# A decoder step on one core: order of work at the tail of the convolution and in the last two output chunks

## What is computed

```
def conv_module(h, hist, w_pw1, b_pw1, w_dw, b_dw, g_ln, b_ln, w_pw2, b_pw2):
    a = h @ w_pw1 + b_pw1
    u = a[..., :D_MODEL] * jax.nn.sigmoid(a[..., D_MODEL:])
    ext = jnp.concatenate([hist.astype(u.dtype), u], axis=1)
    v = depthwise convolution of ext over time, 31 taps, + b_dw
    v = layernorm(v, g_ln, b_ln)
    y = jax.nn.silu(v) @ w_pw2 + b_pw2
    return y, ext[:, -(CONV_WIDTH - 1):]
...
        x = x + squared_relu_mlp(rmsnorm(x, g_ffn[l]), w_up[l], w_down[l])
...
    return rmsnorm(x, g_final), ...
```

## Time and profile before

| what | value |
|---|---|
| median of 3 executions | 1405.34 us |
| the profiled execution, its own time | 1393.17 us |
| its span from first to last instruction | 1391.2 us |
| TensorE busy | 1354.7 us, 97% |
| VectorE busy | 810.8 us, 58% |
| ScalarE busy | 601.3 us, 43% |
| GpSimd busy | 725.7 us, 52% |
| mean granted clock of TensorE | 0.99 of full |

### The profile page before, as it was taken

The page is one execution under the profiler, slowest core; times in us unless marked ns, Lnnn a source line. Parts: engine busy times, 40 slices in busy tenths (PEclk is TensorE's granted clock), DMA queues, the critical chain, the costliest instruction groups (busy, mean ns, idle before and its releaser), DMA issues.

```text
span 1391.2 us, 26303 instructions
## 1 busy us (share of the span) xinstructions
PE 1354.7 (97%) x11048; PEld 1261.1 (91%) x11048; DVE 810.8 (58%) x1232; ACT 601.3 (43%) x1021; POOL 725.7 (52%) x505
## 2 busy tenths in 40 slices
PE   7999889999999999999999999999999999999997
PEld 7877489999999999999899867678999999999997
DVE  6689557655545463766556656554685463645434
ACT  5121255443434443444666544342464444443432
POOL 3321153587878785333323444330437788887831
PEclk9999789999999999999999999999999999999999
DMA  5755302222233324332111477770223322222221
GB/s 215 209 149 147 109 31 92 92 92 91 92 100 100 104 92 147 128 92 66 35 35 53 182 296 261 269 260 7 92 75 101 98 92 92 92 91 92 91 91 65
DMA packets 108356, 160.66 MB, mean 115 GB/s; under 512 B 7696, under 2 KB 93968, under 8 KB 102992
## 3 DMA queue, kind: packets, MB, share of 16 engines
q1 hardware_dynamic: 100688, 116.50, 26.4%
q0 software_dynamic: 7168, 41.95, 8.0%
q10 hardware_dynamic: 384, 0.55, 0.1%
HBM read 146.22 MB, written 4.03 MB: 108 GB/s over the span
## 4 chain that ended last, share of the span: by engine, by line
PE 91%; DVE 4%; ACT 1%; issue 1%; DMA 1%; POOL 1%; ACTq 0%; POOLq 0%; SPq 0%; DVEq 0%
PE ps L1675 31%; PE ps L1805 21%; PE ps L1793 18%; PE ps L1935 5%; PE ps L1975 3%; PE ps L1713 2%; PE ps L2024 2%; PE ps L1726 1%; PE ps L2091 1%; ACT wh L717 1%; PE ps L2005 1%; POOL wl L589 1%; PE ps L2015 1%; PE ps L2033 0%; PE ps L1763 0%
## 5 line engine op out<-in xcount | busy, mean ns | idle before, releaser
L589 POOL TENSOR_TENSOR wl<-raw,wh 128x512 fp32r<-128x512 f32 (+2 forms) x252 | 438.0, 1740 | 441.8 <-ACT wh L717 441.6
L717 ACT ACTIVATE wh<-raw 128x512 fp32r<-128x512 f32 (+2 forms) x253 | 192.6, 762 | 386.3 <-PE ps L1675 184.5
L1675 PE MATMUL ps<-xh,wh 128*128 128x272 f32 x704 | 148.4, 292 | 12.6 <-DVE xl L1084 10.0
L589 POOL TENSOR_TENSOR wl<-wuv,wh 128x512 fp32r<-128x512 f32 x104 | 135.0, 1310 | 48.2 <-ACT wh L717 48.1
L1805 PE MATMUL ps<-mh,wh 128*128 128x272 f32 x768 | 158.7, 288 | 0.0
L1805 PE MATMUL ps<-mh,wl 128*128 128x272 f32 x768 | 158.6, 288 | 0.0
L1805 PE MATMUL ps<-ml,wh 128*128 128x272 f32 x768 | 158.3, 288 | 0.0
L1675 PE MATMUL ps<-xh,wl 128*128 128x272 f32 x704 | 145.6, 289 | 0.0
L1675 PE MATMUL ps<-xl,wh 128*128 128x272 f32 x704 | 145.4, 288 | 0.0
L1675 PEld LDWEIGHTS ps<-xh,wh 128*128 128x128 f32 x704 | 110.6, 190 | 17.7 <-POOL wl L589 9.9
L1805 PEld LDWEIGHTS ps<-ml,wh 128*128 128x128 f32 x768 | 120.4, 188 | 0.0
(11 more groups left out here) (315 smaller groups left out, 3029.3 us busy)
## 6 DMA issues: line engine op xcount, KB each, us to landing
raw<-w_up SPq DMA_DIRECT2D x32, 1024.0 KB, 5.4
raw<-w_down SPq DMA_DIRECT2D x32, 1024.0 KB, 5.1
raw<-w_pw SPq DMA_DIRECT2D x11, 1024.0 KB, 5.8
shifted<-ext SPq DMA_DIRECT2D x112, 66.5 KB, 2.0
raw<-w_o SPq DMA_DIRECT2D x4, 1024.0 KB, 5.7
raw<-w_dq SPq DMA_DIRECT2D x3, 1024.0 KB, 5.4
raw<-w_uq SPq DMA_DIRECT2D x4, 768.0 KB, 4.7
diag<-diags SPq DMA_DIRECT2D x7, 384.0 KB, 3.5
```

Of the source, the lines that this page charges most:

```text
L589: pf.tensor_tensor(weight(wl, u), weight_raw(u), f32(weight(wh, u)), ALU.subtract).then_inc(w_lo, 1)
L717: af.activation(weight(wh, u), weight_raw(u), ACT.Copy).then_inc(w_hi, 1)
L1675: m = tf.matmul(ps[:, bank_of(u) + bank, 0:width], w[:, k, :], a[:, k, part], start=(k == 0 and n == 0), stop=(k == nk - 1 and n == 2))
```

## The change

Five edits. (1) `pe_steps` gives chunk 6 seven steps (28 taps) on TensorE instead of six, so VectorE has three taps left of it. (2) At chunk 7 VectorE does `gates(7)` first, then the taps of chunk 4, then `gated(7)`, then the statistics of chunk 4; ScalarE makes the squares of chunks 4, 5 and 6 after it has issued its shift DMAs, and the next two weight copies after those. (3) TensorE's first sums (`first_sums`) move in front of the last step of chunk 7's taps. (4) The four last halves go in the order (0,0), (0,1), (1,0), (1,1); the column sums of half 0 stand within (1,1), its broadcast after it, and VectorE scales all 8 chunks of half 0 after the last addition. (5) `y` is stored two chunks at a time.

```diff
         def pe_steps(c):
-            return PE_TAPS // GROUPS if c < DC - 1 else STEPS
+            return PE_TAPS // GROUPS + max(c - (DC - LATER), 0)
...
             for h in range(2):
-                for c in range(DC):
-                    sp.wait_ge(y_out, h * DC + c + 1)
-                    sp.dma_start(o_y[:, c, PARTS[h]], yo[:, c, PARTS[h]]).then_inc(s_out, 16)
+                for c in range(0, DC, 2):
+                    sp.wait_ge(y_out, h * DC + c + 2)
+                    sp.dma_start(o_y[:, c:c + 2, PARTS[h]], yo[:, c:c + 2, PARTS[h]]).then_inc(s_out, 16)
...
                 if c == 0:
                     ahead(1)
-                else:
+                elif c < DC - 1:
                     squares_after(c - LATER)
                     ahead(2 * c)
...
-                if c > 0:
+                if 0 < c < DC - 1:
                     ahead(2 * c + 1)
-            squares_after(DC - LATER)
+            for c in range(DC - LATER - 1, DC - 1):
+                squares_after(c)
+            for u in (2 * DC - 2, 2 * DC - 1):
+                ahead(u)
...
                 k = c - LATER
-                if k >= 0:
+                if c == DC - 1:
+                    gates(c)
                     psum_taps(k)
-                    if k == EARLY:
-                        early_mean()
+                    gated(c)
                     statistics(k)
...
+            def first_sums():
+                pe.wait_ge(stat_in, 1)
+                small_part(5, 0, acc)
+                small_part(5, 1, acc2).then_inc(small_mm, 1)
+                mean_part(acc, True, False)
...
                 for k in range(n):
+                    if c == DC - 1 and k == n - 1:
+                        first_sums()
...
             last_x(0, 0)
+            last_x(0, 1)
             last_x(1, 0)
-            last_x(0, 1)
             last_recip(0)
-            dve.wait_ge(y_in, 2 * DC - 2 + 2)
+            last_x(1, 1)
+            dve.wait_ge(y_in, 2 * DC + 1)
             dve.wait_ge(f_mm, 2)
-            outputs(0, range(3))
-            last_x(1, 1)
-            outputs(0, range(3, DC))
+            outputs(0, range(DC))
...
             last_half(0, 0)
+            last_half(0, 1)
             last_half(1, 0)
-            last_half(0, 1)
-            pe.wait_ge(sq_used, SQUARES)
-            column_sums(0, acc, True, False)
-            pe.wait_ge(last_sq, 2)
-            column_sums(0, sq[:, SQUARES % 2, :], False, False)
-            column_sums(0, sq[:, (SQUARES + 1) % 2, :], False, True).then_inc(f_mm, 1)
             last_half(1, 1, DC // 2)
+            broadcast(0)
```

More of the change, by code:

```diff
@@ L575, in _ @@
             for h in range(2):
-                for c in range(DC):
-                    sp.wait_ge(y_out, h * DC + c + 1)
-                    sp.dma_start(o_y[:, c, PARTS[h]], yo[:, c, PARTS[h]]).then_inc(s_out, 16)
-            sp.wait_ge(s_out, 64 + 32 * DC)
+                for c in range(0, DC, 2):
+                    sp.wait_ge(y_out, h * DC + c + 2)
+                    sp.dma_start(o_y[:, c:c + 2, PARTS[h]], yo[:, c:c + 2, PARTS[h]]).then_inc(s_out, 16)
+            sp.wait_ge(s_out, 64 + 16 * DC)
         @block.gpsimd
@@ L788, in _ @@
             load_roots()
-            for c in range(DC - LATER + 1, DC):
-                squares_after(c)
+            squares_after(DC - 1)
             root_in()
@@ L1041, in last_squared @@
             def last_squared(i, h):
-                act.wait_ge(last_in, 2 * h + i + 1)
+                act.wait_ge(last_in, 2 * i + h + 1)
                 af.activation(last_square(i, h), x[:, DC - 2 + i, PARTS[h]], ACT.Square).then_inc(last_sq, 1)
@@ L1053, in _ @@
             act.wait_ge(sq_used, SQUARES)
[L1054 to L1058, removed]
+            for i, h in ((0, 0), (0, 1), (1, 0)):
+                last_squared(i, h)
+                last_scaled(i, h)
             last_root(0)
@@ L1153, in dve_taps @@
                 dst = v[:, c, 0:NP]
-                for k in range(PE_TAPS, TAPS):
+                first = GROUPS * pe_steps(c)
+                for k in range(first, TAPS):
                     w, a = V("w_dw", c * TAPS + k), ext[:, c, k:k + NP]
-                    if k == PE_TAPS:
+                    if k == first:
                         link(df.tensor_scalar(dst, a, w, None, ALU.mult))
@@ L1213, in _ @@
                 k = c - LATER
-                if k >= 0:
+                if c == DC - 1:
+                    gates(c)
                     psum_taps(k)
-                    if k == EARLY:
-                        early_mean()
+                    gated(c)
                     statistics(k)
-                gates(c)
-                gated(c)
+                else:
+                    if k >= 0:
+                        psum_taps(k)
+                        if k == EARLY:
+                            early_mean()
+                        statistics(k)
+                    gates(c)
+                    gated(c)
                 sample_taps(c)
@@ L1618, in last_x @@
             def last_x(i, h):
-                dve.wait_ge(last_mm, 2 * h + i + 1)
+                dve.wait_ge(last_mm, 2 * i + h + 1)
                 xp = x[:, DC - 2 + i, PARTS[h]]
@@ L1702, in run, with mean_part, small_part @@
                         sums()
+            def mean_part(a, begin, end):
+                for h in range(2):
+                    m = tf.matmul(ps[:, 6 + h, 0:HALF], invd[:, :], a[:, h * HALF:(h + 1) * HALF], start=begin, stop=end)
+                return m
+            def small_part(bank, at, a):
+                for j, b in enumerate(blocks5):
+                    m = tf.matmul(ps[:, bank, at + 2 * j:at + 2 * j + 1], a[:, b], invd[:, 0:1], start=True, stop=True)
+                return m
+            def first_sums():
[3 more added lines that the diff above has]
+                mean_part(acc, True, False)
             def tap_products(c):
@@ L1754, in _ @@
             tap_products(DC - 1)
[L1756 to L1769, removed]
             pe.wait_ge(sq_src, DC)
@@ L2088, in last_half @@
                     if k == at:
-                        broadcast(0)
+                        pe.wait_ge(last_sq, 3)
+                        column_sums(0, acc, True, False)
+                        column_sums(0, sq[:, SQUARES % 2, :], False, False)
+                        column_sums(0, sq[:, (SQUARES + 1) % 2, :], False, True).then_inc(f_mm, 1)
                     for n, (w, a) in enumerate(((wh, ah), (wh, al), (wl, ah))):
```

## The result

The changed kernel takes 1409.31 us (median of 15 executions, 1406.73 to 1413.68) against 1403.57 us of the kernel before beside it (15 executions, 1399.15 to 1410.27): ratio 1.0044, 95% interval 1.003 to 1.0057, so +4.2 to +8.0 us about a middle of 6. The medians lie 5.7 us apart. A second measurement of both kernels gave 1.0036 (1.0019 to 1.0053). The forecast was +3.7.

A forecast was written before the change was run, and what follows sets the result against it. The prediction took TensorE, holding 91% of the chain of waits, as the bound: convolution +4.2 us and tail -0.55 us sum to +3.7 us, which on a median of 1405.3 gives 1409.0 us, range 1399 to 1414.

The forecast's parts named there:

- the wait that the forecast was built on: Convolution: VectorE stands until ScalarE's square of chunk 4 is done, 5.5 us lost.
- Gates and shift: Chunk 7: VectorE idles 3.1 us before the gates, ext is written at 139.25, the shift starts 2.5 us earlier.
- The square behind the DMAs: ScalarE's shift issues hold chunk 4's square 6.68 us; VectorE loses 5.5 us; stat_in comes at 161.0, not 156.8.
- The clock: TensorE runs at the lower level from before the first sums; second sums take 4.06 us; convolution +4.2 us.
- My bound of +1.3 for the upper level: Convolution's cost if TensorE's clock stays at its upper level: sums done at 170.8, +1.3 us.
- The rest costs nothing.: From 192 to 1366 us, same instructions in the same order, costed at nothing.
- The tail: Last 25 us: reordered halves and paired stores give -0.55 us, bounds 0 and -1.1.
- Rival 1: TensorE's clock does not fall, or returns at once, in the 5.6 us wait: +0.75 us, 1406.1 us; chance 0.20.
- rival 2: ScalarE's DMA issue does not hold the square: -4.75 us with the tail, 1400.6 us; chance 0.14.
- Rival 3: ScalarE's shift issues take longer than before, 13.7 us for eight: +10.7 us, 1416.0 us; chance 0.10.

The follow-up runs named there:

- e12: The kernel before with only chunk 6's seventh tap step moved to TensorE: 0.9957 (0.9941 to 0.9972), 1394.31 against 1400.27 us.
- e4: The changed kernel, but VectorE adds the square of chunk 4 two steps later: 0.9987 (0.9975 to 1.0000) against the kernel before.
- e11: The changed kernel, but ScalarE squares chunk 4 ahead of its shift DMAs: 0.9984 (0.9968 to 0.9999) against the kernel before.
- e3: The kernel before, unchanged, run again as a control: 0.9995 (0.9979 to 1.0011).
- e9: The kernel before, unchanged, one execution for its profile alone; no ratio given, taken where the kernel before has a median of 1394.3 us.
- e2: The kernel before with only the new order of last halves and the paired stores: 0.9997 (0.9981 to 1.0013).
- e8: The changed kernel itself, measured again: 1.0036 (1.0019 to 1.0053) against the kernel before, 1408.75 us.
- e1: The changed kernel without its last-halves and store edits, so only the convolution's: 1.0044 (1.0028 to 1.0059), 1400.66 against 1393.72 us.
- e5: The changed kernel with the first sums back behind all of chunk 7's taps: 1.0014 (0.9998 to 1.0030) against the kernel before, 1406.55 us.
- e6: The changed kernel with chunk 4's square added later on VectorE and first sums behind all taps: 0.9971 (0.9956 to 0.9986), 1399.87 against 1405.17 us.
- e7: The changed kernel with chunk 6 back at six tap steps on TensorE: 1.0034 (1.0017 to 1.0051) against the kernel before, 1409.04 us.

## Why the prediction was right, and where it was not

The measured +5.7 lies on the side forecast, and the wait that the forecast was built on is there. That the time itself (1409.0 forecast, 1409.3 measured) came out so near is luck: the kernel before had its median 1.8 us lower beside the changed one than in the three executions that I built on, and of the sum's terms one was too large and one was missing. By its steps:

- *Gates and shift.* 3.1 us of idle time forecast, 3.19 measured; `ext` written at 139.25 forecast, 139.85 measured with the trace 0.45 behind. Right. What I did not see is that the second product of chunk 7, done at 137.3, is the floor, the earliest moment at which `gated(7)` can begin: edit 1 alone reaches the same start of the shift (e12), so edit 2's order gained nothing there and cost the stall.
- *The square behind the DMAs.* Right in mechanism, and shown by e4 and e11. Its size: I took ScalarE's eight issues at 6.68 us; they took 5.31, none over 0.80, where the earlier trace rows has one of 1.71. So 4.36 us of stall, not 5.5.
- *The clock.* The lower level from before the first sums: right. First sums 4.42 + 2.02 us against 4.0 + 2.0 forecast, last step 1.91 against 1.7. The step that failed is the second sums: 4.06 forecast, 2.39 measured, because the clock rose meanwhile. My bound of +1.3 for the upper level kept these sums at 4.06, so it was no bound; with the first sums at the lower level and the second at the upper, the same sum gives +2.4, and the trace has them done 2.15 us later without the 0.45. The convolution thus cost 1.9 us at the pair's start, 2.7 by the product after it, where I had said 4.2. But one profile of each kernel is a poor measure of this: the second sums took 4.06, 2.48, 2.83 and 2.72 us in the four with the old convolution (before, e3, e9, e2), and 2.39, 2.39 and 4.43 in the three with all of edits 1 to 3 (after, e8, e1). The pair starts at 179.7, 180.4 and 180.7 in these three, and at 173.3 to 177.4 in the four, the profile of before being the latest; the means, 180.3 and 175.0, lie 5.3 us apart. I also read the lower level of the earlier trace rows together with the wait ahead of the taps; e12 has it in the sums without such a wait, so the wait is not needed for it.
- *"The rest costs nothing."* This was wrong: 2 to 5 us more between the pair and the key transposes, with the half clock there. That term was put at nothing because the instructions are the same, and their order does not tell at which clock they run. In the number it made up for the other's oversize.
- *The tail.* -0.55 forecast. The pairs land in 2.4 us, exactly the forecast, and at an equal clock in the second broadcast the new tail is 0.6 us shorter than the old: right. In the two profiles compared first it came to nothing, since the broadcast ran at the lower level in the changed kernel, 1.50 for 0.87 us. I had not priced the clock in this place; e1 shows that it can fall here with the old tail too.
- *Rival 1* (upper level) fell by the 0.50 of the stretches; *rival 2* (the issue does not hold the square) by the 4.36 us wait. Its price of -4.75 us (0.9966) was on the large side even for a kernel whose square stands ahead: e11 is at 0.9984 (0.9968 to 0.9999), though its shift leaves ScalarE's queue later. *Rival 3* fell: the issues took less, not longer.
- *Edit 3.* I priced it within the sum and took it as given; e5 shows that it costs 2 us with the stall, and the traces of e4 and e6 that it costs without it.

## What to carry to other kernels

Before moving an engine's step past a group of DMA issues on its queue, count the issues as work: eight of them held ScalarE for 5.3 us, and who waits for the step behind them waits as long. When an order is changed to let something start sooner, look for the next floor under it first (here a product done at 137.3): the smallest edit that reaches the floor, four taps moved to TensorE, gave the whole start and measured 6 us faster, and no run with the reordering measured better. Try each edit alone. And take the price of a step that can run at either clock from more than one profile: the same 20 records cost 2.5 to 4.1 us in four profiles of the old convolution.

## What was not expected of the hardware

TensorE's granted clock fell in places where it had never fallen before an earlier edit elsewhere: in ten of ten profiles with an edited convolution against none of four, with 2 to 5 us more in the stretch of some 615 us behind it. It also stood at its lower level while TensorE ran small sums without a pause (e12, 158 to 168 us). And the DMA issues of chunk 7 do not all take the 0.6 us of most: in the four profiles with the old convolution each of the two queues has one slow shift issue (ScalarE 0.95 to 2.10 us, SyncE 1.25 to 1.76). In the ten with an edited one no shift issue takes over 0.84 us, but in five of them (after, e1, e4, e6, e7) SyncE's issue of the diagonals takes 1.4 to 2.0 us; in e8, the same kernel as after, it takes 0.58. So the order alone does not decide which issue is slow.
